# Two-block sequence model on one core: the second chunk's own products of the first conditioning moved between the transposes of the input, with VectorE's part summed in columns of its own

## The reference, cut to what matters

```
c_act = silu(c)                                   # one vector of 1024
cond  = c_act @ ada_w[0] + ada_b[0]               # 3072 values
shift = cond[:1024]; scale = cond[1024:2048]; gate = cond[2048:]
h     = rmsnorm(x, norm_g[0]) * (1 + scale) + shift
proj  = h @ lru_in_w                              # 1024 x 2048
```

## Time and profile before

| what | us |
|---|---|
| median of 3 runs (2252.01 to 2252.19) | 2252.01 |
| the profiled execution, its own time | 2253.6 |
| the span of the profiled execution | 2251.7 |
| TensorE busy in the span | 2169.7 (96%) |
| VectorE busy | 1338.7 (59%) |
| ScalarE busy | 600.0 (27%) |
| GpSimd busy | 204.7 (9%) |

### The profile page before, as it was taken

One profiled execution on the slowest core, in us unless ns is written; L12 is line 12 of the kernel. 1 busy time (PEld: TensorE's weight loads), 2 busy tenths in 40 slices (PEclk: granted clock), 3 DMA queues, 4 the chain that ended last, 5 costly groups with the idle time before them and its releaser, 6 DMA issues. The chain is left out here.

```text
span 2251.7 us, 20632 instructions
## 1 busy us (share of the span) xinstructions
PE 2169.7 (96%) x7066; PEld 1110.0 (49%) x7066; DVE 1338.7 (59%) x1851; ACT 600.0 (27%) x972; POOL 204.7 (9%) x151
## 2 busy tenths in 40 slices
PE   6999999999999999999999999999999999999998
PEld 5444444346656656656454454544444444444443
DVE  4687743264764764755823577357469999426533
ACT  4345522223443443433212420121100000122011
POOL 0000000122212213212100000000000000003200
PEclk8999999999999999999999999999999999999999
DMA  9333330121101111111410325331111110113021
GB/s 326 113 109 117 114 123 0 75 53 40 44 23 35 43 27 33 44 30 33 138 33 19 122 51 65 67 93 33 38 42 33 43 37 24 52 45 124 19 93 56
DMA packets 200910, 146.86 MB, mean 65 GB/s; under 512 B 49996, under 2 KB 171905, under 8 KB 200833
## 3 DMA queue, kind: packets, MB, share of 16 engines
q1 hardware_dynamic: 186417, 144.14, 21.8%
q10 hardware_dynamic: 14048, 0.85, 0.4%
q0 software_dynamic: 384, 1.05, 0.2%
HBM read 126.45 MB, written 18.38 MB: 64 GB/s over the span
## 5 line engine op out<-in xcount | busy, mean ns | idle before, releaser
L2130 PE MATMUL bank<-hT,ring 128*128 128x512 f32 x1472 | 638.9, 595 | 2.9 <-DMA ring<-in_w_in 2.9
L2130 PEld LDWEIGHTS bank<-hT,ring 128*128 128x128 f32 x1472 | 280.6, 191 | 353.8 <-issue 349.8
L2838 DVE SCALAR_TENSOR_TENSOR yT<-s_arena,yT 128x1024 f32<-128x1024 f32 x240 | 308.3, 1285 | 8.4
L1235 PE MATMUL bank<-hT,ring 128*128 128x512 f32 x336 | 157.1, 593 | 1.8 <-ACT silu_z L1464 1.8
L1809 DVE SCALAR_TENSOR_TENSOR memory<-memory,col_exp_last,bank 128x128 f32<-128x128 f32 x64 | 22.2, 348 | 153.8 <-PE bank L1409 153.8
L2130 PE MATMUL bank<-ssm_y,ring 128*128 128x512 f32 x192 | 83.9, 593 | 0.6 <-DVE s_arena L2852 0.6
L1235 PEld LDWEIGHTS bank<-hT,ring 128*128 128x128 f32 x336 | 58.5, 191 | 49.4 <-issue 49.4
L1235 PE MATMUL bank<-resid,yT 128*128 128x512 f32 x168 | 82.5, 593 | 0.0
L2468 ACT ACTIVATE s_arena<-bank 128x1024 f32<-128x1024 f32 x8 | 8.2, 1023 | 242.5 <-PE bank L2130 242.5
L1772 DVE SCALAR_TENSOR_TENSOR buf_c<-bank,buf_c 128x512 f32<-128x512 f32 x32 | 22.1, 692 | 82.5 <-PE bank L1321 79.7
L2827 DVE TENSOR_TENSOR s_arena<-bank,s_arena 128x1024 f32<-128x1024 f32 x8 | 9.8, 1226 | 94.6 <-ACT s_arena L2468 94.6
(11 more groups left out here) (554 smaller groups left out, 3482.6 us busy)
## 6 DMA issues: line engine op xcount, KB each, us to landing
ring<-in_w_in SPq DMA_DIRECT2D x48, 512.0 KB, 3.9
ada<-in_ada_w SPq DMA_DIRECT2D x8, 2048.0 KB, 8.1
ring<-in_gdn_in_w SPq DMA_DIRECT2D x32, 512.0 KB, 4.1
resid<-in_x SPq DMA_DIRECT2D x8, 1024.0 KB, 9.1
ring<-in_lru_in_w SPq DMA_DIRECT2D x16, 512.0 KB, 3.9
lru_arena<-in_ada_w SPq DMA_DIRECT2D x6, 1024.0 KB, 12.3
x_scratch<-resid SPq DMA_DIRECT2D x2, 2048.0 KB, 10.7
decayT<-g_scratch SPq DMA_DIRECT2D x8, 512.0 KB, 4.3
```

What stands on the lines that cost most here:

```text
L1235: last = nc.tensor.matmul(bank[:, to, :], w[:, k, :], v[:, k, :], start=(first and k == 0), stop=(k == KB - 1), skip_group_check=not only)
L2130: last = nc.tensor.matmul(bank[:, 2 * PAIR[name] + h, :], w[:, k, :], src[:, k, h * HALF:(h + 1) * HALF], start=(k == 0), stop=(k == kt - 1))
L2838: dve_b.mark(dve.scalar_tensor_tensor(out=yT[:, n, :], in0=padded[:, p, j:j + S], scalar=taps[:, p, j:j + 1], in1=yT[:, n, :], op0=ALU.mul ...
```

## The change

TensorE now does five flips, then its own products for chunk 2 (four slices in each of four column groups, into columns 4 to 7 of bank 0, closed there), then the last three flips, then chunk 0 as before, and then the four products of VectorE's part of chunk 2 with ones, which go to columns 8 to 11 of bank 0. The step `chunk2` is marked on the last of them. VectorE gets one more instruction in part 0 of the modulation: it adds columns 8 to 11 to the scale. Chunks 1 and 3 keep the old function.

```diff
@@
+            scale_summed = sem("first_scale")
             ON_DVE = {0: KT, 2: 4, 1: KT, 3: 6}
@@
-                    for t in range(TT):
+                    for t in range(5):
                         flip(t)
-                    act_a.wait(pe, "vecs0")
+                    act_a.wait(pe, "c_act")
+                    pe.wait_ge(chunk_loaded[2, 1], 16)
+                    for m in range(4):
+                        for k in range(ON_DVE[2], KT):
+                            nc.tensor.matmul(bank[:, 0, 4 + m:5 + m], first_chunks[2][:, k, m * P:(m + 1) * P], c_act[:, k:k + 1],
+                                             start=(k == ON_DVE[2]), stop=(k == KT - 1))
+                    for t in range(5, TT):
+                        flip(t)
                     chunk(0, 0)
-                    chunk(2, 0)
+                    dve_a.wait(pe, f"w2_{ON_DVE[2] - 1}")
+                    for m in range(4):
+                        last = nc.tensor.matmul(bank[:, 0, 8 + m:9 + m], weighted[:, 1, m * P:(m + 1) * P], ones[:, 0:1], start=True, stop=True)
+                    pe_a.mark(last, "chunk2")
                     pe.wait_ge(rows_loaded[1], 16 * len(other_rows))
@@
                         dve_a.wait(dve, f"sums{part}")
+                        if part == 0:
+                            dve.tensor_tensor(both[:, 1], both[:, 1], bank[:, to, 8:12], ALU.add).then_inc(scale_summed, 1)
+                            dve.wait_ge(scale_summed, 1)
                         dve_a.mark(dve.scalar_tensor_tensor(out=both[:, 1], in0=both[:, 1], scalar=1.0, in1=vec("norm_g0", 4 * part, 4),
                                                             op0=ALU.add, op1=ALU.mult), f"cond{part}")
```

## The result

The changed kernel took 2256.15 us (median of 13 runs, 2254.09 to 2261.36), the kernel before 2252.19 us in the same comparison (13 runs). The ratio is 1.0016 with a 95% interval of 1.0008 to 1.0023: 3.6 us slower, by 1.8 to 5.2. That is inside what was called "within 0.2%", and clear of no change all the same. The profiled execution took 2254.84 us with a span of 2252.9, so it is one of the quicker ones of this kernel.

A forecast was written before the change was run, and what follows sets the result against it. It took TensorE, busy 96% of the span, as the bound, so start delays persist: a 0.9 us later first large product, worth +0.6 us, gave 2254.2 against the profiled 2253.6, or 2252.6 us against the median 2252.01; range 2248.8 to 2255.8.

The forecast's parts named there:

- step 1: After the fifth flip, TensorE waits for chunk 2's second half to land: 1.1 us idle, until 25.0 us.
- Step 2: 32 own products from 25.0 us: 17 at the high clock, 15 at the low after a fall at 26.9; over at 30.1.
- Step 3: Last three flips, 24 transposes from 30.1 us: 15 at the low clock, rise at 33.2, 9 at the high; over at 34.2.
- Step 4: 16 products with ones after the flips, 1.76 us plus landing: VectorE's sum starts at 36.1 against 35.38, 0.7 us later.
- Step 5: VectorE's added addition puts 0.2 us on the path; first large product 0.9 us later, at 39.2.
- Step 7: VectorE's chunks 1 and 3 end later, at 48.6 us, still 2.9 us before TensorE wants them; nothing else moves.
- forecast case: The main case, chance 0.55: 2252.6 us, with bounds of about 2251.5 to 2254.0 from the clock's fall and rise.
- The base of the sum: One profiled execution of the kernel before, 2253.6 us, first large product at 38.31; the median lies 1.6 us below it.
- Step 6: Large products starting 0.9 us late cost 0.45 to 0.9 us at the end, depending on the clock's rise; taken as +0.6.
- A: Rival: clock stays high through own products and flips, large products 2.2 us early; 2249.2 us, chance 0.22.
- B: Rival: flips do not bring the clock back, large products 3.5 us late; 2255.5 us, or 2257.2 with early fall; chance 0.16.
- C: Rival: shifts at the start are swallowed later and do not reach the end; 2252.0 us, chance 0.07.

The follow-up runs named there:

- landed_chunk: Changed kernel with the own products taken from chunk 0 instead of chunk 2, removing the landing wait (wrong scale); 2254.29 against 2251.78 us, ratio 1.0010.
- before_look2: The kernel before, unchanged, in a further single execution for a third profile; 2254.95 us.
- own_behind_flips: Changed kernel with chunk 2's own products moved behind all eight flips and chunk 0; 2250.23 against 2253.4 us for before, ratio 0.9988; again 0.9987.
- transposes_instead: Changed kernel with the 32 one-column own products replaced by 32 128-column transposes (result incomplete); 2252.8 against 2251.78 us for before, ratio 0.9998.
- changed_again: The changed kernel, unedited, measured and profiled a second time; 2256.49 against 2253.4 us for before, ratio 1.0020.

## Why the prediction was right or wrong

**What held.** The direction did, and the range only just: slower, inside 2248.8 to 2255.8 by the ratio (2252.01 x 1.0016 = 2255.6; the raw median of the later comparison, 2256.15, is against a before of 2252.19). The edge is 0.2 us away and the interval, 2253.8 to 2257.2, reaches beyond it, so that the range held is in part luck. The first profile came out close to what was written: step 1, idle from 23.75 to 24.74, forecast 23.85 to 25.0. Step 2: products over near 28.8, forecast 30.1. Step 3: flips over near 34, forecast 34.2. Step 4: sum at 36.15, forecast 36.1. Step 5: +0.20 us, forecast 0.2. Large products at 39.27, forecast 39.2. Step 7: VectorE's chunk 3 ended at 44.68 + 3.97 = 48.65, forecast 48.6, and TensorE wanted it at 52.42. Part of this agreement is luck too. The own products were over 1.3 us sooner than forecast, as the clock happened to rise at 24.4, and the flips took 5.2 us and not 4.1, as it rose late; the two errors cancel at 34. The forecast had the clock high at 23.85 and falling at 26.9; it was low there and fell at 27.8. The other two profiles put the first large product 2.6 and 2.0 us later than forecast.

**What failed is the size**, +0.6 us forecast, +3.6 (1.8 to 5.2) measured. The range of the forecast case, up to 2254.0, does not hold it. Two terms were mis-sized.

- *Step 2, the clock at the start of the own products.* I took it as high there, with 17 of 32 instructions at 0.11 us, since it was high at 23.5 in the one profile of before. In two of three profiles of the changed kernel it was low already and all 32 ran at 0.21 us: 6.96 us instead of 5.1. The reason is the interruption itself, as the two pairs of profiles above show: with flips 5 to 7 moved away, only 16 transposes stand ahead of the one-column products, and in these two executions the clock did not return in them. In changed (rise at 24.4) and in landed_chunk (24.0) it did return just behind them, so 16 are enough in one execution and not in another. I had costed the interruption for the flips behind it, never for those before it.
- *Step 3, the rise.* I put it 3.1 us after the flips resume, the shortest case; it came after 5.8 (28.78 to 34.62), 4.8 and 3.8 us.
- *The base of the sum.* The earlier trace rows show one clock history of the kernel before. Its two other profiles put the first large product at 36.76 and 39.13. The forecast compared one history with one; the comparison that counts is between the averages, 38.07 and 40.73. Of the 2.7 us there, 0.2 is the addition. The wait (0.99, 0.90 and 1.65 us, 1.2 on average) is made up for by the gap before VectorE's part that is now filled (1.14, 0.83 and 1.74 us, 1.2 on average). What is left, about 2.5 us, is one-column work and flips at the low clock.

**Step 6** said that a late start is worth between half and all of it, with 0.45 as the low end. (The middle of 0.45 and 0.9 is 0.68; I had written 0.6.) At the product near 75 us the averages are 73.83 and 76.59: 2.8 us, all of the 2.7. At 1270 us they are 1270.68 and 1272.40, 1.7 us apart, but that is not the start's doing alone. before_look2 was the first of the three at 75 us and no longer at 1270, as it met the low clock again in between: PEclk is 0.83 between 410 and 420 us and 0.76 between 1215 and 1222, where the first profile of before shows 1.00. With a scatter of over 2 us in each kernel, the share that is left at 1270 us is not known from three profiles each.

**The rivals.** A (clock high throughout) was seen in none of three profiles. B was near in size (2255.5, against 2255.6 by the ratio) and half right in mechanism. It costed all 24 transposes at the low clock, 5.1 us; they took 5.36, 5.15 and 4.68. By its own condition, a rise later than 5 us after the flips resume, the first profile (5.8 us) is a case of it and the other two (4.8 and 3.8) are not, though these two have the fall ahead of the own products that B named as an addition. Where it was wrong is behind the flips: the clock was back at 34.6, 36.6 and 35.5, and the products with ones ran high for the most part (1.29 and 1.03 us in changed) and not low throughout (3.4 us). C is refuted by own_behind_flips: 2 to 3 us at the start do reach the end. The Trainium skill's statement in "TensorE: Matmul & The Clock Gate", Part 4, that transposes do not count for the clock, is contradicted for these float32 transposes once more by transposes_instead, where the clock rose at 28.6 after nothing but transposes since 24.9. The same page of the Trainium skill, in "Part 1: The HAM clock gate", says of the clock's window that it is free-running and that its phase varies from run to run. The further profiles of both kernels agree in that the changes of the clock fall at other moments each time, and I should have weighed that in the base of the sum.

The cause is settled as far as this: the place of the own products costs (own_behind_flips against the changed kernel, disjoint intervals), and it costs because one-column products stand there and not transposes (transposes_instead, whose interval lies below both of the changed kernel). How the loss divides between the wait, the clock and the addition is read from profiles and not separated by times.

## What to carry to other kernels

In this kernel one-column products were cheap filler where TensorE was idle and no wide work waited behind them; put between two runs of transposes they cost both of them the clock. Before moving work into a gap, compare the landing of its data with the gap: here the gap behind chunk 0 (27.3 us) took the same 32 instructions for a gain of 2.8 us. And where the clock's changes fall at other moments in each execution, take more than one profile of the kernel before as the base of a sum of a few microseconds.

## What the runs showed of the hardware that was not expected

- The clock's history differs between executions of one and the same kernel: first fall at 20.1, 21.5 and 29.2 us for the kernel before, and a first large product between 36.76 and 39.13.
- 16 transposes (3.65 us at the low clock) followed by one-column work left the clock at 0.50 in changed_again; with 32 transposes in place of that work it rose (transposes_instead, at 28.6).
- The clock rose at 24.4 in the changed kernel while TensorE stood idle, and fell at 21.0 in the middle of transposes: its changes need not fit the instruction that is running.
- An instruction of a one-column product takes 0.214 us at 0.50 and 0.11 us at 1.00, though only one column moves, and a 128-column transpose about 0.21 and 0.11: the clock prices both alike.
- The wait for the scratch transfer near 1370 us varied from 0.42 to 7.05 us between executions.
